# Last tile of an output projection mixed, turned and squared in pieces, with its row shift moved from VectorE to GpSimd

## The reference, cut to what matters

```python
x = x + g1 * (y @ w_out)                       # per token 1024 columns
h = modulate(rms_norm(x, norm_ffn_g[l]), sh2, sc2)   # h * (1 + scale) + shift
scores = jax.nn.sigmoid(h @ router_w)          # (tokens, 16)
biased = scores + router_b
grouped = biased.reshape(..., 4, 4)            # best group by the sum of its two best, then its two best experts
w = w / jnp.sum(w)                             # weights of the two
out = sum over experts of combine * ((silu(h @ w_gate) * (h @ w_up)) @ w_down)
x = x + g2 * out
```

## Time and profile before

| | |
|---|---|
| median of 3 runs | 1579.54 us (1579.3 to 1580.94) |
| the profiled execution | 1578.25 us |
| its span, first to last instruction | 1576.6 us |
| mean granted TensorE clock | 0.986 |
| PE busy | 1506.4 us (96%) |
| DVE busy | 704.4 us (45%) |
| ACT busy | 332.8 us (21%) |
| POOL busy | 118.8 us (8%) |
| DMA | 370.24 MB, mean 235 GB/s |

### The profile page before, as it was taken

How to read it: one execution, slowest core, us unless ns; L and a number is a source line. 1 busy time by engine, 2 the same in 40 slices (tenths; PEclk the granted TensorE clock), 3 DMA queues, 4 the chain that set the end, 5 groups by cost and what they waited for, 6 DMA issues and landing times. The chain is left out here.

```text
span 1576.6 us, 23833 instructions
## 1 busy us (share of the span) xinstructions
PE 1506.4 (96%) x9898; PEld 1023.3 (65%) x9898; DVE 704.4 (45%) x1420; ACT 332.8 (21%) x769; POOL 118.8 (8%) x101
## 2 busy tenths in 40 slices
PE   5999999999999999899999999999999999899995
PEld 2765644766677768775546648786678887655563
DVE  1497777577775442732221135336534312512122
ACT  2121244322223110210101023225322211100001
POOL 0100000032212210000000030000000000000000
PEclk9999999999999999999999999999999999999998
DMA  9575411333544589489999984431134376899997
GB/s 372 203 239 166 156 54 43 119 133 124 158 147 160 173 286 358 173 322 391 400 394 392 402 314 147 138 97 45 38 111 146 121 283 266 343 426 428 419 411 296
DMA packets 128364, 370.24 MB, mean 235 GB/s; under 512 B 14269, under 2 KB 91351, under 8 KB 107516
## 3 DMA queue, kind: packets, MB, share of 16 engines
q1 hardware_dynamic: 118588, 344.86, 58.8%
q10 hardware_dynamic: 5936, 13.09, 2.3%
q0 software_dynamic: 3728, 10.71, 1.9%
HBM read 361.66 MB, written 12.98 MB: 238 GB/s over the span
## 5 line engine op out<-in xcount | busy, mean ns | idle before, releaser
L1247 PE MATMUL ps<-hT,ring 128*128 128x512 f32 (+1 forms) x544 | 207.6, 535 | 0.0
L1250 PE MATMUL ps<-ring,hT 128*128 128x256 f32 (+1 forms) x832 | 173.1, 364 | 3.7 <-DVE arena L2242 2.3
L1250 PEld LDWEIGHTS ps<-ring,hT 128*128 128x128 f32 x832 | 147.0, 190 | 27.5 <-issue 10.3
L1247 PEld LDWEIGHTS ps<-hT,ring 128*128 128x128 f32 x544 | 101.3, 191 | 86.9 <-issue 81.7
L1446 PE MATMUL ps<-arena,ring 128*128 128x512 f32 (+1 forms) x384 | 136.3, 486 | 0.0
L1596 PE MATMUL ps<-arena 128*32 128x128 f32 (+2 forms) x1104 | 102.4, 342 | 0.7 <-DVE arena L2554 0.7
L1596 PE MATMUL ps<-ring,arena 128*64 128x256 f32 (+1 forms) x1280 | 93.9, 334 | 3.8 <-DMA ring<-in_w_exp_gate 2.1
L1446 PEld LDWEIGHTS ps<-arena,ring 128*128 128x128 f32 x384 | 72.4, 190 | 31.7 <-issue 24.6
L2856 POOL DMA_INDIRECT arena<-moe_rows,idx_i x23 | 22.8, 991 | 897.8 <-DVE idx_i L2622 512.9
L1381 PE MATMUL ps<-hT,ring 128*128 128x256 f32 x384 | 87.9, 379 | 0.6 <-ACT arena L1903 0.6
L1159 PE MATMUL ps<-ring,arena 128*128 128x256 f32 x384 | 85.9, 380 | 2.5 <-DVE arena L2420 2.5
(11 more groups left out here) (310 smaller groups left out, 1962.5 us busy)
## 6 DMA issues: line engine op xcount, KB each, us to landing
ring<-in_w_in SPq DMA_DIRECT2D x54, 1024.0 KB, 6.2
ring<-in_w_ada SPq DMA_DIRECT2D x48, 1024.0 KB, 5.3
arena<-in_w_exp_down SPq DMA_DIRECT2D x18, 2048.0 KB, 16.1
arena<-in_w_exp_up SPq DMA_DIRECT2D x15, 2048.0 KB, 15.8
ring<-in_w_exp_down SPq DMA_DIRECT2D x14, 2048.0 KB, 13.7
ring<-in_w_exp_gate SPq DMA_DIRECT2D x12, 2048.0 KB, 16.4
ring<-in_w_exp_up SPq DMA_DIRECT2D x12, 2048.0 KB, 15.0
hT<-in_w_exp_gate SPq DMA_DIRECT2D x10, 2048.0 KB, 15.7
```

What stands on the lines that cost most here:

```text
L1247: last = pe.matmul(ps[:, bank, 0:tok.stop - tok.start], w[:, k, at:at + width], hT[:, k, tok], start=(k == 0), stop=(k == KD - 1))
L1250: last = pe.matmul(ps[:, bank, 0:width], hT[:, k, P * tok:P * (tok + 1)], w[:, k, at:at + width], start=(k == 0), stop=(k == KD - 1))
```

## The change

- `mix` of the last tile's second half goes in two pieces of 256 columns; the two quarters' products lie in different banks, and `wo_ready` is raised after each. `turn_x` and `keep_x` of that half become `turn_last` and `keep_last`, two blocks each. The first two transposes stand inside the last product, ahead of its last two blocks. The last two stand behind six of the eight blocks of the last tile's router.
- ScalarE squares 768 columns of the last tile when its first piece is mixed, and the other 256 later; the two sums meet in the root's bias (`mean_of_most`, VectorE).
- The last tile's router parts are kept by VectorE (`keep_last_parts`), not by ScalarE.
- A tiny square root ahead of `keep_x`, and a tiny sigmoid behind the last root, make ScalarE load each table there.
- `shift_rows` of every tile moves to GpSimd. For it the scaled rows of all tiles but the last go to the free tile behind in `h_toks` and not to `mix_tmp`. The shift of the last tile waits only for its scaled rows, and no `mix` waits for a shift. `order_experts` waits for the last shift.
- VectorE's order for the last two tiles is written out.

The semaphore counts follow: `halves` and `turned_halves` count one more per layer. The diff, cut:

```diff
+        def rows_scaled(l, t):
+            return h_toks[l][:, t + 1, :] if t < NT - 1 else mix_tmp
@@ TensorE
+                def turn_last(piece):
+                    pe.wait_ge(x_mixed, halves(l, 2 * nq[l] + piece))
+                    if piece:
+                        pe.wait_ge(h2_dve, turned_halves(l, 1))
+                    else:
+                        pe.wait_ge(h2_act, 2 * before(nq, l) + nq[l])
+                    for k in range(2):
+                        last = pe.transpose(ps[:, 0 if piece else nq[l] - 1, P * k:P * (k + 1)],
+                                            res[:, NT - 1, P * (4 + 2 * piece + k):P * (5 + 2 * piece + k)], ident)
+                    last.then_inc(h2_turned, 1)
...
+                            if ends and quarter:
+                                pe.wait_ge(x_mixed, v + l)
+                            bank = 4 + (v + (ends and quarter)) % 2
+                            for k in range(KD):
+                                if ends and quarter and k == KD - 2:
+                                    turn_last(0)
+                                last = pe.matmul(ps[:, bank, COLS * quarter:COLS * (quarter + 1)], yT[l][k][:, P * t:P * (t + 1)],
+                                                 w[:, k, :], start=(k == 0), stop=(k == KD - 1))
+                            if ends and not quarter:
+                                last.then_inc(wo_ready, 1)
...
-                turn_x(NT - 1, 1)
                 add_parts(NT - 2)
-                router(NT - 1)
+                router(NT - 1, range(6))
+                turn_last(1)
+                router(NT - 1, range(6, KD))
                 add_parts(NT - 1)
@@ ScalarE
+                def squares_of_most():
+                    nonlocal sq
+                    act.wait_ge(x_mixed, halves(l, 2 * nq[l]))
+                    act.wait_ge(sq_ready, sq)
+                    act.activation(junk2[:, 0:768], res[:, NT - 1, 0:768], ACT.Square, accum_out=ss_most[:, 0:1]).then_inc(sq_ready, 1)
+                    sq += 1
...
+                act.activation(root[:, :], eps[:, :], ACT.Sqrt)
                 for t in range(t0, NT):
                     keep_x(t)
                 for t in range(t0, NT):
-                    squares(ready, junk2, t, t + 1)
+                    if t == NT - 1:
+                        squares_of_most()
                     if t > t0:
                         keep_parts(t - 1)
-                keep_parts(NT - 1)
+                    if t < NT - 1:
+                        squares(ready, junk2, t, t + 1)
+                squares_of_last()
+                act.activation(root[:, :], eps[:, :], ACT.Sigmoid)
@@ VectorE
+                def mean_of_most():
+                    dve.wait_ge(sq_ready, sum(NT + q + 1 for q in nq[:l]) + NT + nq[l])
+                    dve.tensor_scalar(ss_most[:, 1:2], ss_most[:, 0:1], 1.0 / D, EPS, ALU.mult, ALU.add).then_inc(consts_made, 1)
...
-                    if half and t > t0:
-                        dve.wait_ge(h2_ready, before(nq, l) + t - t0)
...
+                    root_of(t)
                     scale_rows(t, 0)
-                    scale_rows(t, 1)
-                    if t < NT - 1:
-                        shift_rows(t)
+                    if t < NT - 2:
+                        scale_rows(t, 1)
+                mix(NT - 1, 1, 0)
+                keep_x(NT - 2)
+                scale_rows(NT - 2, 1)
+                if NT - 3 >= t0:
+                    scale_logits(NT - 3)
+                mean_of_most()
+                keep_last(0)
+                mix(NT - 1, 1, 1)
+                keep_last(1)
+                scale_logits(NT - 2)
+                keep_last_parts()
+                dve.wait_ge(x_mixed, halves(l, 2 * nq[l] + 1))
+                root_of(NT - 1)
+                scale_rows(NT - 1, 0)
+                scale_logits(NT - 1)
+                scale_rows(NT - 1, 1)
...
-                shift_rows(NT - 1)
@@ GpSimd
+            def shift_rows(l, t):
+                by_row = lambda a: a.rearrange("p (q k) -> p q k", k=KD)
+                if t > first_tile(l):
+                    pool.wait_ge(h2_ready, before(nq, l) + t - first_tile(l))
+                pool.wait_ge(consts_made, scalings(l, t - first_tile(l) + (2 if t == NT - 1 else 1)))
+                pool.tensor_tensor(h_toks[l][:, t, :].rearrange("p (k q) -> p q k", k=KD), by_row(rows_scaled(l, t)),
+                                   by_row(ffn_rows[l][t // XT][1]), ALU.add).then_inc(h2_ready, 1)
             for l in range(DEPTH):
                 pool.dma_start(list_d.rearrange("(p n) o -> p (n o)", p=P), no_token[:, :]).then_inc(zeroed, 16)
+                for t in range(first_tile(l), NT):
+                    shift_rows(l, t)
```

More of the change, by code:

```diff
@@ L65 @@
 STEPS = 7
+CONSTS = 4
 X_BANK, Z_BANK, B_BANK = 1, 5, 0
@@ L498, in trunk, with scalings, halves, turned_halves @@
         nq = [NT - first_tile(l) for l in range(DEPTH)]
+        def scalings(l, n):
+            return CONSTS + turned_halves(l, n)
+        def halves(l, n):
+            return 2 * before(nq, l) + l + n
+        def turned_halves(l, n):
+            return before(nq, l) + l + n
         def roots(l, n):
@@ L1141, in _ @@
                 sp.nop()
-            sp.wait_ge(x_mixed, 2 * before(nq, DEPTH))
+            sp.wait_ge(x_mixed, halves(DEPTH, 0))
             sp.wait_ge(h2_ready, before(nq, DEPTH))
@@ L1485, in turn_x, with keep_busy, router @@
                     last.then_inc(h2_turned, 1)
[L1487 removed]
+                def keep_busy(n, bank=0):
                     for _ in range(n):
[L1490 to L1492 removed]
+                        pe.matmul(ps[:, bank, 0:P], ident, ident, start=True, stop=True)
+                def router(t, ks=range(KD)):
                     i = t - t0
[L1495 removed]
+                    if i > 0 and ks[0] == 0:
                         pe.wait_ge(h2_act, 2 * before(nq, l) + nq[l] + i)
[L1497 to L1502, removed]
+                    for k in ks:
+                        if k == 0:
+                            pe.wait_ge(h2_act, 2 * before(nq, l) + i + 1)
+                        elif k == 4:
+                            pe.wait_ge(h2_dve, turned_halves(l, i + 1))
+                        elif k == 6 and t == NT - 1:
+                            pe.wait_ge(h2_dve, turned_halves(l, i + 2))
                         c = k % 4
@@ L1521, in _ @@
                         v = 2 * before(nq, l) + nq[l] * half + t - t0
+                        ends = half and t == NT - 1
                         if v >= 2:
-                            pe.wait_ge(x_mixed, v - 1)
+                            pe.wait_ge(x_mixed, v - 1 + l)
                         for quarter in range(2):
@@ L2478, in scale_rows @@
                     cols = slice(512 * half, 512 * (half + 1))
[L2479 to L2483, removed]
-                    dve.tensor_tensor(h_toks[l][:, t, :].rearrange("p (k q) -> p q k", k=KD), by_row(mix_tmp),
-                                      by_row(ffn_rows[l][t // XT][1]), ALU.add).then_inc(h2_ready, 1)
+                    ins = dve.scalar_tensor_tensor(out=rows_scaled(l, t)[:, cols], in0=res[:, t, cols], scalar=rstd[:, t:t + 1],
+                                                   in1=ffn_rows[l][t // XT][0][:, cols], op0=ALU.mult, op1=ALU.mult)
+                    if half:
+                        ins.then_inc(consts_made, 1)
                 def compare(out, values):
```

61 lines of the change are left out of this document (38 added, 23 removed).

## The result

| | before | after |
|---|---|---|
| median, same job | 1580.19 us (13 runs, 1579.3 to 1581.4) | 1584.06 us (13 runs, 1582.2 to 1586.7) |
| profiled execution / its span | 1578.25 / 1576.6 us | 1583.04 / 1581.4 us |
| ratio after to before | | 1.0025, 95% interval 1.0017 to 1.0033 |

The kernel became 0.25% slower, and 1584.06 us lies outside the predicted range of 1571.8 to 1583.0. Medians of before moved between 1579.8 and 1581.5 us from one job to the next, so experiments are compared by their ratio to before in their own job.

The account below looks back on a forecast made before the run. Small waits bound each layer's chain from output projection to the first expert's rows, and DMA the end. Layer 0 -0.1, layer 1 -1.25 and DMA -0.7 summed to -2.05: 1577.5 us beside the median, range 1571.8 to 1583.0.

Parts of the forecast that it names:

- D: Time of one `shift_rows` on GpSimd, taken as 2.35 us, with 3.7 us as the upper end.
- Rival 1: GpSimd's strided store is slower, 3.7 us per shift, delaying comparisons in both layers: +5.2, so 1582.7 us; chance 0.17.
- The lock: GpSimd's shifts block VectorE operations with two SBUF inputs; the last shift holds up the comparisons by 2.35 us per layer.
- Rival 3: GpSimd's shifts do not hold up VectorE's small comparisons in the chain: 1572.3 us; chance 0.20.
- Layer 1's chain: Layer 1, output projection to first expert: followers 2.55 us earlier, shift +2.35, shift behind `assign` gone -1.05; -1.25 in all.
- the -0.1: Layer 0's sum: followers of the sigmoid 1.4 us earlier, shift beside comparisons +2.35, shift ahead of the places gone -1.05.
- The clock: Forecast kept layer 1's two row groups at full clock, despite TensorE waiting some 2.5 us longer for `assign`.
- Rival 2: Longer TensorE waits halve the clock in one layer 1 row group, +1.6, and lose 0.7 of DMA: 1579.8 us; chance 0.21.
- behind a similar pause: Argument against the clock falling: layer 1's two row groups ran at full clock before, after a similar pause.
- The DMA credit of 0.7: Layer 1: last tile's store and next gate weights go out earlier, leaving less DMA work at 1359; 0.7 us gain.
- The other edits cost nothing: Tiny activations, one 128x1 operation, the wait in `order_experts` and GpSimd's gathers were to add no time.

Follow-up runs that it names:

- experiment 9: Kernel before with one unused buffer of 2 columns ahead of `arena`, which then starts 32 bytes further on; ratio 1.0005.
- experiment 13: Kernel before with 8 unused columns ahead of every buffer, putting four of the five large ones off multiples of 64 bytes; ratio 1.0012.
- experiment 14: Kernel before with unused columns so that all five large buffers start at multiples of 64 bytes; ratio 1.0005.
- experiment 5: Kernel after with 24 filler products in layer 1 only, 10 in layer 0; 1578.70 us, ratio 0.9989.
- experiment 1: Kernel after with 24 instead of 10 filler products ahead of `assign` in both layers; 1577.62 us, ratio 0.999.
- experiment 10: Kernel after with `ss_most` allocated behind `arena`, so that `arena` is back at its old address; ratio 1.0010.
- experiment 2: Kernel after with only the last tile's shift of each layer back on VectorE, behind `assign`; 1581.63 us, ratio 1.0016.
- experiment 3: Kernel after with GpSimd's last shift in layer 1 cut to 8 of 1024 columns; 1581.26 us, ratio 1.0005.
- experiment 6: Kernel after with the last tile's shift back on VectorE, 18 and 16 fillers ahead of `assign` and 8 behind the places; 1576.65 us, ratio 0.9979.
- experiment 11: Kernel after with 24 fillers in both layers and `ss_most` allocated behind `arena`; ratio 0.9975.
- experiment 16: Kernel after with all shifts on VectorE, 16 fillers, 8 behind the places, and all five large buffers at multiples of 64 bytes; ratio 0.9971.
- experiment 7: Kernel after with all six shifts back on VectorE, 16 fillers in both layers and 8 behind the places; 1576.89 us, ratio 0.998.

## Why the prediction was wrong, point by point

- **D, the price of a shift on GpSimd: right.** 2.37 us, where 2.35 was taken and 3.7 was the upper end. Rival 1 is dead. The Trainium skill, page "GPSIMD Engine Reference", section "7. Performance pitfalls for Q7 kernels", prices strided reads only, and this strided write cost nothing measurable (2.37 beside 2.35 in a row).
- **The lock: right in kind and size.** Comparisons of 2.42 us (layer 0) and 2.35 us (layer 1) ended with GpSimd's shift. It is the rule of the Trainium skill's page "SBUF — State Buffer", section "🔬 SBUF: two separate sides", and this trace agrees with it. Rival 3 is dead. One detail was wrong: `mean_of_most`, a `tensor_scalar` on SBUF, was to wait for GpSimd in layer 0, and it took 0.14 us at 655.54, inside the shift of 653.51 to 655.89. The one of 1.03 us in the earlier trace rows, on two columns in place of one, did end with a GpSimd sum (353.49 + 1.03 = 354.52, beside 353.24 + 1.27 = 354.51); what makes the difference is open.
- **Layer 1's chain: right.** From the end of the last product to the followers 4.95 us were worked out (1338.75 to 1343.7), and 5.14 measured (1337.80 to 1342.94). From there to the use of the places 5.8 were worked out and 5.4 measured. Counted from the start of the projection, the followers came 2.57 earlier (2.55 predicted) and the places were used 1.71 earlier (1.25 predicted for the first expert).
- **Layer 0: a little better than the -0.1.** This execution reached layer 0's projection 1.45 us later (591.75, before 590.30), so I count from there. The followers came 1.9 earlier (1.4 predicted), the first rows 0.4 earlier, and the first expert's gate 2.2 earlier, since the first row group ran partly at full clock: 5.20 us in place of 6.98. That part need not be a gain of the change, for with before's chain and ten fillers the same group took 3.81, 5.44 and 7.00 us in experiments 9, 13 and 14. Fillers in layer 0 did not matter in the sum (experiment 5).
- **The clock: here the prediction failed.** Its forecast held layer 1's rows at full clock. Rival 2 named the place, the cause and the 1.6 us per group: 3.51 + 3.65 against 2.00 + 1.98 is 1.5 and 1.7. But it priced one group and 0.7 of DMA, 1579.8 us in all. Both groups fell (+3.2), the fillers behind the places (+0.7) and the first gate (5.58 against 3.67, +1.9): 5.8 us at the half clock. Experiment 1 gives the same 5.8 from the projection to the request, with nothing changed but the fillers. The chain's own gain of 1.7 comes off that, and TensorE frees the slot 4.1 us later.
- **The argument that kept its chance at 0.21** was that both groups ran at full clock before "behind a similar pause". The pause was not similar. Before, the clock had fallen at 1342.5 and 20 filler passes at 0.50 lay between that fall and the rows; TensorE was busy from 1345.06 to `assign`. The prediction moved those fillers 3 us forward and left TensorE idle behind them without asking what they had been doing. The rows to read were the fillers' line and the clock from 1343 to 1349; the 0.71 of 1347 to 1351 in the earlier trace rows was the tail of that stretch, and the prediction passed it by.
- **The DMA credit of 0.7: turned into a loss.** DMA did run on from 1347 to 1351 (349 GB/s, where 12 had been), and was through at 1359. But the credit assumed that TensorE's first expert comes earlier, and it came later. Over the 18 profiled kernels of this study the span grows by 0.8 us for each microsecond by which the next gate weights are asked for later (1355.1 to 1366.0; correlation 0.88, single kernels up to 2.7 us off the line; part of it is that some executions reach layer 1 later). In layer 1 the end follows this request.
- **"The other edits cost nothing": doubtful.** The two columns of `ss_most` move `arena` by 32 bytes, and DMA's rate behind the first expert went from 422 to 416 GB/s with it (experiments 9 and 10). The prediction had no term for that; its price in time is open.
- **The range** reached to 1583.0 for the sake of rival 1 (1582.7), which had nothing to do with the cause. With the clock's fall priced through the gate, 5.8 in place of 1.6 and no DMA credit, rival 2 would have stood at 1577.5 + 5.8 + 0.7 = 1584.0. That this is the measured median is in part luck: the sum has no term for the place of `arena`, and it starts from 1579.54 where before had 1580.19 in the job of the result.

## What to carry to other kernels

Filler products are part of the schedule: when the work ahead of them gets shorter, or when they run at full clock, the same number covers about half the time, and the critical work behind them pays. Before you shorten a chain that TensorE waits for, read the granted clock over the wait and count how far the fillers reach. And price a fall of the clock to the first point where it showed full speed again (here through the rows and into the first gate, to 1360.5), not over the next group alone.

Two executions of the same code reach a stretch at different times: the profiled ones lie up to 3.2 us apart at layer 0's projection, ahead of all that the change touches. So measure a change from the last event that it does not touch. And a small buffer put ahead of a large one moves the large one: keep the addresses when you compare, or try them on their own.

## What the runs showed of the hardware

- With the clock down, TensorE being busy did not bring it back quickly for these products: in the kernel after it was busy from 1347.97 on and the clock stood at 0.50 until 1360.5. In the kernel before it was back at 1349.3, 4 us after dense fillers began.
- Idle times of 1.67 and 1.68 us ahead of the places were followed by the fall in the traces of experiments 2 and 3, one of 0.71 was not (experiment 1). That is what these runs did; where the border lies was not tried. The code alone does not settle it: in experiments 6, 11 and 16 the clock fell at 1342.0, 1344.2 and 1340.4, about where the fillers begin, and in 1 and 7 it did not fall there, with the same TensorE code up to that point. So fillers have two jobs, and there they brought it back (48 passes in 7.08 us in 11, in 5.61 at full clock in 1).
- GpSimd writes 1024 elements per partition 128 apart in 2.37 us, as fast as in a row (2.35), where VectorE takes 1.95 against 1.23. It still holds up VectorE's operations with two inputs in SBUF for all of it.
- With every queue full (1370 to 1550 us) DMA moved 421 to 423 GB/s in the six kernels whose `arena` starts at byte 128512 of each partition, and 415 to 418 in the twelve where it starts 32 or 64 bytes further on.
